# Two transformer blocks on one core: the high weight tiles multiplied twice with 256 columns instead of once with 512, and another placement of the operands modulo 256 bytes

## The reference

```python
# first block
z = rms_norm(h, g) @ w_in                      # 2048 x 5120: q, k, v, and the two gMLP halves
mixed = concat(diff_attention(...), gmlp_gate(...))
h = h + mixed @ w_out
f = rms_norm(h, g2)
h = h + (silu(f @ ffn_w1) * (f @ ffn_w3)) @ ffn_w2          # hidden 5632
h = h + (p @ pl_w_up) * sigmoid(h @ pl_w_gate)
# second block, on 16 meta tokens and the 256
proj = rms_norm_2(h) @ w_in                    # 2048 x 12288: pool, three convolution parts, two gates
y_a = causal_multiscale_pool(u) @ pool_w * pool_scale
y_b = (gb * causal_depthwise_conv(gc * v)) @ conv_out_w
h = h + (g_a * y_a + g_b * y_b) @ w_o
h = h + (silu(f @ w_gate) * (f @ w_up)) @ w_down
return rms_norm_2(h)
```

## Time and profile before

| | us |
|---|---|
| median of 3 runs (2665.45 to 2666.21) | 2665.51 |
| the profiled execution's own time | 2665.68 |
| its span, first to last instruction | 2663.6 |
| PE busy | 2652.8 (100%) |
| PEld busy | 2347.5 (88%) |
| DVE busy | 1658.5 (62%) |
| ACT busy | 1236.0 (46%) |

### The profile page before, as it was taken

One profiled execution on the slowest core, in us unless ns is written; L12 is line 12 of the kernel. 1 busy time (PEld: TensorE's weight loads), 2 busy tenths in 40 slices (PEclk: granted clock), 3 DMA queues, 4 the chain that ended last, 5 costly groups with the idle time before them and its releaser, 6 DMA issues.

```text
span 2663.6 us, 39872 instructions
## 1 busy us (share of the span) xinstructions
PE 2652.8 (100%) x15711; PEld 2347.5 (88%) x15711; DVE 1658.5 (62%) x1645; ACT 1236.0 (46%) x1355; POOL 0.8 (0%) x7
## 2 busy tenths in 40 slices
PE   9999999999999999999999999999999999999998
PEld 8889888888888888888999999888888888888887
DVE  6567766555565556795676666556765645564555
ACT  5456554444444444565443443444554434443444
POOL 0000000000000000000000000000000000000000
PEclk9999999999999999999999999999999999999999
DMA  8554555655656555555555555555565555565553
GB/s 291 184 174 145 195 189 193 193 193 188 198 181 205 181 199 189 185 191 191 176 175 189 181 184 182 190 182 190 189 205 189 189 189 189 189 198 192 180 192 138
DMA packets 254251, 502.92 MB, mean 189 GB/s; under 512 B 8130, under 2 KB 11652, under 8 KB 253988
## 3 DMA queue, kind: packets, MB, share of 16 engines
q1 hardware_dynamic: 252180, 497.61, 56.6%
q10 hardware_dynamic: 1952, 3.68, 0.4%
HBM read 498.37 MB, written 2.88 MB: 188 GB/s over the span
## 4 chain that ended last, share of the span: by engine, by line
PE 99%; DVE 0%; ACT 0%; DMA 0%; issue 0%; ACTq 0%; DVEq 0%
PE ps L1359 49%; PE ps L1373 24%; PE ps L1392 4%; PE ps L1394 4%; PE ps L1393 4%; PE ps L1412 4%; PE ps L1411 4%; PE ps L1410 3%; PE ps L1403 0%; PE ps L1402 0%; PE ps L1404 0%; PE ps L1322 0%; DMA xtok<-in_x_dram 0%; PE ps L1547 0%; PE ps L1545 0%; PE ps L1546 0%
## 5 line engine op out<-in xcount | busy, mean ns | idle before, releaser
L825 DVE TENSOR_TENSOR lo<-raw,hi 128x1024 fp32r<-128x1024 f32 x940 | 1127.8, 1223 | 852.2 <-ACT hi L491 843.6
L491 ACT ACTIVATE hi<-raw 128x1024 fp32r<-128x1024 f32 x940 | 971.5, 1055 | 1061.2 <-PE ps L1373 483.6
L1359 PE MATMUL ps<-A,hi 128*128 128x512 f32 x3648 | 862.8, 393 | 0.0
L1359 PEld LDWEIGHTS ps<-A,hi 128*128 128x128 f32 x3648 | 675.6, 188 | 140.4
L1359 PE MATMUL ps<-B,hi 128*128 128x512 f32 x1984 | 477.5, 394 | 0.0
L1373 PEld LDWEIGHTS ps<-A,lo 128*128 128x128 f32 x3648 | 438.0, 188 | 12.0
L1373 PE MATMUL ps<-A,lo 128*128 128x256 f32 x3648 | 439.9, 277 | 0.0
L1359 PEld LDWEIGHTS ps<-B,hi 128*128 128x128 f32 x1984 | 365.3, 188 | 74.8
L1373 PEld LDWEIGHTS ps<-B,lo 128*128 128x128 f32 x1984 | 246.1, 188 | 10.0
L1373 PE MATMUL ps<-B,lo 128*128 128x256 f32 x1984 | 247.8, 279 | 0.0
L1412 PE MATMUL ps<-B,lo 128*128 128x258 f32 (+1 forms) x768 | 219.4, 286 | 0.0
(11 more groups left out here) (240 smaller groups left out, 1342.6 us busy)
## 6 DMA issues: line engine op xcount, KB each, us to landing
raw<-in_w_in_dram SPq DMA_DIRECT2D x136, 1024.0 KB, 5.1
raw<-in_ffn_w_dram SPq DMA_DIRECT2D x132, 1024.0 KB, 5.1
raw<-in_w_gate_up_dram SPq DMA_DIRECT2D x88, 1024.0 KB, 5.0
raw<-in_w_down_dram SPq DMA_DIRECT2D x44, 1024.0 KB, 5.1
raw<-in_w_out_dram SPq DMA_DIRECT2D x16, 1024.0 KB, 5.2
raw<-in_pl_w_gate_dram SPq DMA_DIRECT2D x16, 1024.0 KB, 5.1
raw<-in_conv_out_w_dram SPq DMA_DIRECT2D x16, 1024.0 KB, 5.1
raw<-in_w_o_dram SPq DMA_DIRECT2D x16, 1024.0 KB, 5.1
```

Source lines behind the costliest of these rows:

```text
L491: act.activation(hi[:, slot % RING], raw[:, raw_slot, 2 * (slot % 2):2 * (slot % 2) + 2, :], ACT.Copy).then_inc(hi_ready, 1)
L825: dve.tensor_tensor(lo[:, slot % RING], raw[:, slot // 2 % RAWS, 2 * (slot % 2):2 * (slot % 2) + 2, :], hi[:, slot % RING], ALU.subtract). ...
L1359: last = pe.matmul(ps[:, b0 + m, :], high(slot, kk, m), both, start=j == 0 and kk == 0, stop=ends and j == seg.pieces - 1 and kk == 1)
```

## The change: single passes of 256 columns, one accumulator, another placement

1. `highs` multiplies each high weight tile twice with 256 columns, first with the high, then with the low activations, both into the first half of the bank. All 16 products of a piece's high tiles keep an LDWEIGHTS of their own; within a row of tiles the four tiles come with the high activations and then the same four with the low ones.
2. So a bank holds the whole sum, and the copy by ScalarE and the addition by VectorE go (`copy_second`, `add_halves`, the semaphore `copied`). VectorE's first operation of a group now reads PSUM itself and frees the banks (`free_sums`); ScalarE waits for `psum_free` (`wait_group`).
3. `ln_stats` moves from between `hi` and `lo` to behind `sumsq`, so that `A` begins 192 past `hi` and 192 past `lo` modulo 256, and the columns of `B` for "halves" and "wide_halves" with it. `TOKEN_AT` goes from `META + 32` to `META + 16`: in the layout "token" the columns of `B` begin at the same remainder as both rings. In "token" segments that read `A` (`v`, `g`) the moving weights begin 64 past the stationary tile for both rings; before it was 192 for `hi` and 64 for `lo`.
4. The first scores wait for `psum_free` of the last `qk` group instead of a semaphore of their own.

```diff
-TOKEN_AT = META + 32
+TOKEN_AT = META + 16
...
         hi = sb("hi", [P, RING, 2, GC], F32R)
-        ln_stats = sb("ln_stats", [P, 32])
         lo = sb("lo", [P, RING, 2, GC], F32R)
 
+        rstd_meta = sb("rstd_meta", [P, META])
         tiny = sb("tiny", [P, 2, TM])
-        rstd_meta = sb("rstd_meta", [P, META])
         A = sb("A", [P, KT, 2 * T], F32R)
...
         sumsq = sb("sumsq", [P, 2, T])
+        ln_stats = sb("ln_stats", [P, 24])
...
-            def copy_second(kind, G, end, b0):
-
-                act.wait_ge(pieces_used, end)
-                act.wait_ge(psum_free, G)
-                if SQUARED & {kind, before[0]}:
-                    wait(ready)
-                before[0] = kind
-                act.activation(pb_copy[:, :, :], ps[:, b0:b0 + 4, T:2 * T], ACT.Copy).then_inc(copied, 1)
+            def wait_group(G):
+
+
+                act.wait_ge(psum_free, G + 1)
+                act.nop(nofuse=True)
...
-            def add_halves(G, b0, to):
-                second.skip()
-                wait(second)
+            def sums_done(end):
+
+                dve.wait_ge(pieces_used, end)
                 wait(given)
                 wait(ready)
-                dve.tensor_tensor(to, ps[:, b0:b0 + 4, 0:T], pb_copy[:, :, :], ALU.add).then_inc(psum_free, 1)
+
+            def free_sums(ins, G):
+
+                ins.then_inc(psum_free, 1)
                 dve.wait_ge(psum_free, G + 1)
...
                 elif kind in ("gate", "ga", "gbr"):
-                    add_halves(G, b0, work[:, :, :])
-                    hand(dve.tensor_tensor(work[:, :, :], work[:, :, :], Rm, ALU.mult))
+                    sums_done(end)
+                    free_sums(dve.tensor_tensor(work[:, :, :], sums, Rm, ALU.mult), G)
...
                 elif kind == "part":
                     hk = some(h, k, 4, 0, T)
-                    add_halves(G, b0, work[:, :, :])
-                    step(dve.tensor_tensor(hk, hk, work[:, :, :], ALU.add))
+                    sums_done(end)
+                    free_sums(dve.tensor_tensor(hk, hk, sums, ALU.add), G)
...
                 X = activations(buf, layout)
+                at = 0 if layout == "halves" else META
                 pe.wait_ge(hi_ready, n + 1)
                 for kk in range(2):
                     k = 2 * j + kk + (4 * WIDEST_FIRST[g] if seg.name == "pool" else 0)
-                    for m in range(MT):
-                        both = X[:, k, 0:2 * T] if layout == "halves" else X[:, k, META:META + 2 * T]
-                        last = pe.matmul(ps[:, b0 + m, :], high(slot, kk, m), both, start=j == 0 and kk == 0,
-                                         stop=ends and j == seg.pieces - 1 and kk == 1)
+                    for part in range(2):
+                        x = X[:, k, at + part * T:at + (part + 1) * T]
+                        for m in range(MT):
+                            last = pe.matmul(ps[:, b0 + m, 0:T], high(slot, kk, m), x, start=j == 0 and kk == 0 and part == 0,
+                                             stop=ends and j == seg.pieces - 1 and kk == 1 and part == 1)
```

More of the change, by code:

```diff
@@ L132 @@
 PER = {
[L133 to L136, removed]
+    "res_ffn": (2, 0, 2, 1), "part": (0, 0, 0, 0), "gate": (0, 0, 1, 0), "up": (0, 1, 1, 1),
+    "plgate": (5, 2, 4, 1), "ga": (0, 0, 1, 0), "gbr": (0, 0, 1, 0), "cv": (1, 0, 0, 0),
+    "cg": (5, 0, 0, 0), "cb": (0, 1, 1, 1), "cout": (0, 1, 1, 1), "res_ffn2": (3, 0, 2, 1),
+    "tpart": (0, 0, 0, 0),
 }
@@ L191, in turns_of @@
 def turns_of(eng, seg, tallies, run, lead=0):
-    per = [sum(PER.get(kind, (0,) * 5)[i] for kind in seg.kinds) for i in range(5)]
+    per = [sum(PER.get(kind, (0,) * 4)[i] for kind in seg.kinds) for i in range(4)]
     whole = seg.turns if seg.turns == 1 else min(seg.turns, max(seg.peel, lead))
@@ L390, in bass_two_blocks @@
         PLUP = next(s for s in SEGS if s.name == "plup")
+        QK = next(s for s in SEGS if s.name == "qk")
         def landed(n):
@@ L556, in evacuate @@
                     return
[L557 to L560, removed]
+                if kind in ("qk", "plup", "pool"):
+                    return
+                more()
+                if kind == "part":
                     return
                 if kind in ("res_ffn", "res_ffn2"):
-                    asked.skip()
-                    wait_alone(asked)
+                    wait(ready)
+                    wait_group(G)
                     given.mark(act.activation(pb_copy[:, :, :], some(h, k, 4, 0, T), ACT.Square))
@@ L849, in residual_out @@
                 hk = some(h, k, 4, 0, T)
-                hand(dve.tensor_tensor(hk, hk, work[:, :, :], ALU.add))
                 meanwhile()
@@ L892, in evacuate @@
                     hk = some(h, k, 4, 0, T)
-                    add_halves(G, b0, work[:, :, :])
-                    step(dve.tensor_tensor(hk, hk, work[:, :, :], ALU.add))
+                    sums_done(end)
+                    free_sums(dve.tensor_tensor(hk, hk, sums, ALU.add), G)
                     more()
                 elif kind == "res_gate":
-                    add_halves(G, b0, work[:, :, :])
+                    hk = some(h, k, 4, 0, T)
+                    sums_done(end)
+                    free_sums(dve.tensor_tensor(hk, hk, sums, ALU.add), G)
                     if gi < MT - 1:
@@ L909, in evacuate @@
                 elif kind in ("up", "cb"):
-                    add_halves(G, b0, work[:, :, :])
-                    step(dve.tensor_tensor(work[:, :, :], work[:, :, :], Rm, ALU.mult))
+                    sums_done(end)
+                    free_sums(dve.tensor_tensor(work[:, :, :], sums, Rm, ALU.mult), G)
                     if kind == "up":
@@ L918, in evacuate @@
                 elif kind == "cout":
-                    add_halves(G, b0, work[:, :, :])
-                    step(dve.tensor_tensor(work[:, :, :], work[:, :, :], some(G2, k, 4, 0, T), ALU.mult))
+                    sums_done(end)
+                    free_sums(dve.tensor_tensor(work[:, :, :], sums, some(G2, k, 4, 0, T), ALU.mult), G)
                     hand(dve.tensor_tensor(work[:, :, :], work[:, :, :], some(G1, k, 4, 0, T), ALU.add))
@@ L968, in evacuate @@
                 elif kind == "pool":
-                    add_halves(G, b0, work[:, :, :])
+                    sums_done(end)
                     for i in range(MT):
-                        last = dve.scalar_tensor_tensor(out=G1[:, k + i, :], in0=work[:, i, :], scalar=gain("pscale", k + i),
+                        last = dve.scalar_tensor_tensor(out=G1[:, k + i, :], in0=ps[:, b0 + i, 0:T], scalar=gain("pscale", k + i),
                                                         in1=G1[:, k + i, :], op0=ALU.mult, op1=ALU.mult)
-                    step(last)
+                    free_sums(last, G)
                 elif kind in ("cv", "cg"):
@@ L1299, in last @@
                         dve.tensor_scalar(HT[:, a, c:e], HT[:, a, c:e], r, None, ALU.mult).then_inc(left_scaled, 1)
-            walk(dve, {0: own, 1: asked, 2: given, 3: ready, 4: second}, split, evacuate, side, last)
+            walk(dve, {0: own, 1: asked, 2: given, 3: ready}, split, evacuate, side, last)
         @block.tensor
```

37 lines of the change are left out of this document (17 added, 20 removed).

## The result

The changed kernel takes 2678.99 us (median of 5 runs, 2678.94 to 2679.24) against 2665.51 before: 13.5 us more, a ratio of 1.0051 with a 95% interval of 1.0040 to 1.0062. It is slower, by more than the 0.2% that can be told apart. The forecast was 2641, faster; the time lies in the range, on the wrong side of the kernel before.

The account below looks back on a forecast made before the run. TensorE was taken as the bound, the time being the sum of its steps. From the profiled execution, 2665.68 - 27 + 75 x 0.05 - 1.5 = 2640.9, so 2641 us; range 2630 to 2703.

Parts of the forecast that it names:

- The two steps: TensorE's start-to-start step for 256 columns: 113.4 ns in the short pace, 117.8 in the long one.
- the formula: Time change over all weight tiles: -27 + 75 s us, breaking even at s = 0.36.
- s: Share of weight tiles running in the long pace, taken as 0.05.
- The changes of kind: Switches between highs and lows, where differing offsets can shift the pace; one offset removes this, so a pace should hold.
- Rival A: Run beginnings behind breaks lock into the long pace, s near 0.9: 2706 us; chance 0.24.
- Rival B: Each stretch keeps its pace: about 2659 us; beside it mixtures, s 0.15 to 0.5, 2650 to 2676; together 0.26.
- Rival C: TensorE cannot take in twice the instructions so densely: 2664 us at 115 ns, 2713 at 117.8; chance 0.08 with anything unthought of.
- the rule of the Trainium skill: Fixed 2.5 ns per matmul: 5664 more would cost 14 us, giving about 2680 us.
- Rival D: Offsets of moving columns past the rings have no effect; forecast stays 2641 us, with B then likelier; no separate chance.
- Tokens: "Token" segments reading `B`, 1056 matmuls: 0 taken, ends -3.9 and +5.4 us.
- `u`: Segment of 384 matmuls of 256 columns, all at 192 now: gain of 1.5 us counted.
- "Conv" and "wide": "Conv" segments, 1536 matmuls of 258 columns: 0 taken, lower end -8 us, upper as far above; "wide" got no term.

Follow-up runs that it names:

- kick_short: The changed kernel with one matmul cut in two inside a stretch already at the short pace (`f2_up0`, 13th piece): 2679.84 us.
- kick_1: The changed kernel with one 256-column matmul cut into two of 128, in the first feed-forward's piece right behind the break at 363 us: 2651.13 us.
- split_only: The changed kernel with the placement of before (highs 64, lows 192 past their ring), highs still two matmuls of 256 columns: 2642.0 us.
- all_64: The changed kernel with `A` and `B` beginning 64 past both rings: 2706.4 us.
- kick_3: kick_1 with two more matmuls cut, in the first pieces of `f2_up1` and `f2_up2` in the second feed-forward: 2637.46 us.
- zero_256: The changed kernel with offsets of 0 for both rings, by padding alone: 2746.3 us.
- hi0_512: The kernel before (highs of 512 columns) with highs at offset 0 and lows at 192: 2669.71 us.

## Why the prediction was wrong

**The bound, and what hides the rest: right.** TensorE without waits, the group ends worth nothing, the clock full, 186 to 200 GB/s with a DMA share of 0.6: all as forecast. The two steps were right as well, and so was the formula: with the measured s of 0.60, -27 + 75 x 0.60 = +18 against +16.0 for these segments.

**The step that failed: the choice of s.** "For equal offsets I lean to the short pace: there no step is lost at all (3.63 us for 32), so nothing pushes it out ... I take s = 0.05." The premise held for the changed kernel: no short stretch left its pace, and in `kick_short` not even a kick moved one. The conclusion did not follow. No long stretch of the changed kernel left its pace either, and which one a stretch gets is settled at its beginning: 0.60 of the matmuls were long, not 0.05. With 3.8 us lost for each 0.05 of s, the one beginning at 363 us was worth 32 us (7199 x 4.4 ns): had it fallen the other way, the change would have been some 18 us faster than before (`kick_1`, in which `plup` and most of `plgate` stayed long, is 14 us faster). The rows had said so: of two beginnings at hand one was short and one was long. I should have made the shares of these the forecast, and given the longest stretch, 706 us without a break, a chance of its own of about one half. The forecast would then have been two cases 32 us apart, not one of 2641.

**The changes of kind: the sign was wrong.** I counted their removal as a gain. `split_only` keeps them and is 37 us faster than the change. At 64 / 192 they throw long runs back into the short pace (in most places, not in `plgate`). With one offset for both, as in the changed kernel, they do nothing.

**Rival A** had the mechanism right ("one beginning sets the pace for all up to the next") and only the share too high for this placement, 0.9 against 0.60. `all_64` is A's case at another offset, 2706.4. **Rival B**, stretches that keep their old pace, is refuted by the third and fourth row of the stretches, which changed places; the time fell just above its mixtures. **Rival C** is refuted by `split_only` and by `kick_3`, in which all but some 450 of the 16992 matmuls run at 113.4. So the rule of the Trainium skill that was weighed with it ("TensorE: Matmul & The Clock Gate", Back-to-back issue gap; 2.5 ns fixed for each matmul, a formula that the section gives for the gap of a matmul by itself and not for a stream with weight loads) does not describe these matmuls: at 192 / 192 two steps of 256 columns in the short pace take 226.7 ns and one of 512 takes 233.4, and at 0 the order is the other way, 240.0 against 227.0. That its 2680 us lies 1 us from the measured time is luck: `split_only` has the same number of matmuls and takes 2642. **Rival D**, that the placement does nothing, is refuted by `zero_256` against `all_64` and the changed kernel: 2746, 2706 and 2679 us from padding alone. The sentence of the Trainium skill (the same page, step 1 of its account of a matmul) that loading the next weights doesn't steal read bandwidth from the running matmul is hard to square with that: for TensorE, the only thing that padding changes is where the moving columns lie relative to the loaded weights (and which addresses are read). That it is the two reads that meet is argued and not shown.

**The small terms.** Tokens: 0 taken, -4.2 measured, the lower end of my bounds (-3.9). `u`: -1.5 taken, -0.2 measured. "Conv" and "wide": 0 taken, +2.4.

**What stays open.** What a beginning must have to fall into the short pace: the cut matmuls, which lose 0.11 us each, ended in it in all four places, but the waits at 1112 us ended in either, and no run here predicts the outcome of the other breaks. Why changes of kind at 64 / 192 rescue most long runs and not that of `plgate`; why in `hi0_512` the lows all fall to the long pace beside highs at 0; and why 128 has 118.7. I did not measure the pattern of the kicks as a function of their length.

## What to carry to other kernels

Where TensorE is dense and its steps are the bound, read them from start to start, by stretch, and look for two levels of the same instruction: the difference (here 4.4 of 113.4 ns, up to 4% of the time) is neither a cost of the instruction nor of its number, and a mean or a busy time hides it. A change of shape or placement then redraws which level each stretch gets, so a forecast has to be a set of cases, one for each long stretch, and two parts of a change must be timed apart, since their effects don't add. Once the paces are known, one small disturbance behind a bad beginning can be worth more than the change: three matmuls cut in two turned 13.5 us of loss into 28 us of gain, though such a kick was tried in this kernel and at this offset alone, and will have to be looked at again after every other edit.

## What the hardware showed that I had not expected

- The same instruction sequence on the same buffers has two lasting paces, 113.4 and 117.8 ns for 256 columns. The long one held for 7199 matmuls, and one matmul cut in two, just behind its beginning, ended it (2678.99 to 2651.13 us). The cut loses 0.11 us, and the short pace stands four steps behind it.
- The step depends on where the moving columns begin against the ring of weights, modulo 256 bytes; four offsets were tried, 64 bytes apart. With highs and lows alike and 256 columns: 120.0 ns at 0; 113.4 or 117.8 at 64 and at 192; 118.7 or 120.0 at 128. For 512 columns: 227.0 at 0, 228.9 or 233.3 at 64 (before), 233.4 at 192.
- Two matmuls of 256 columns are not dearer than one of 512: 226.7 against at best 227.0 ns for the highs (226.7 in the "token" segments), each with a weight load of its own (PEld busy 97% in the changed kernel, 88% before).
- What is best for one kind can be worst for its neighbour: at 0 the 512 columns have their best step and the 256 their worst.
